# A token mixer and expert kernel on one core: the results of experts 0 to 6 go through DRAM rows instead of one-hot products

## What is computed

```python
def moe_swiglu(x, router, w1, w3, w2):
    logits = (xt @ router).astype(jnp.float32)
    top_val, top_idx = lax.top_k(logits, TOP_K)           # 2 of 8
    gate = jax.nn.softmax(top_val, axis=-1)
    combine = einsum("tk,tke->te", gate, one_hot(top_idx, 8))
    for e in range(8):
        out = out + combine[:, e:e+1] * swiglu(xt, w1[e], w3[e], w2[e])
    return out
# afterwards: h = layer_norm(ALPHA * h + out), which is the result
```

## Time and profile before

| | |
|---|---|
| median of three runs | 1586.84 us (1585.2 to 1588.51) |
| span of the profiled execution, which is its own time from first to last instruction | 1584.4 us |
| TensorE matmul busy | 1543.7 us, 97% |
| VectorE busy | 1342.3 us, 85% |
| ScalarE busy | 964.6 us, 61% |
| GpSimd busy | 47.1 us, 3% |
| moved by DMA | 446.33 MB, 282 GB/s over the span |

### The profile page before, as it was taken

The page is one execution under the profiler, slowest core; times in us unless marked ns, Lnnn a source line. Parts: engine busy times, 40 slices in busy tenths (PEclk is TensorE's granted clock), DMA queues, the critical chain, the costliest instruction groups (busy, mean ns, idle before and its releaser), DMA issues.

```text
span 1584.4 us, 18355 instructions
## 1 busy us (share of the span) xinstructions
PE 1543.7 (97%) x7468; PEld 1225.3 (77%) x7468; DVE 1342.3 (85%) x1437; ACT 964.6 (61%) x1001; POOL 47.1 (3%) x34
## 2 busy tenths in 40 slices
PE   7999999999999999999999999999999999999997
PEld 5565589989666677888888888888888888888885
DVE  8999667766599768888889989889998988998897
ACT  3233465644112537777777677677677677677775
POOL 0111000000021000000000000000000000000000
PEclk9999999999999999999999999999999999999999
DMA  8132545653442557999889999989999989999981
GB/s 338 62 151 80 213 177 200 252 205 116 186 159 80 194 205 301 377 375 359 350 345 366 359 369 365 354 340 368 356 367 372 355 340 372 369 369 371 363 334 52
DMA packets 41819, 446.33 MB, mean 282 GB/s; under 512 B 4472, under 2 KB 4728, under 8 KB 8576
## 3 DMA queue, kind: packets, MB, share of 16 engines
q1 hardware_dynamic: 39504, 438.78, 71.1%
q10 hardware_dynamic: 2224, 6.31, 1.1%
HBM read 439.81 MB, written 5.26 MB: 281 GB/s over the span
## 4 chain that ended last, share of the span: by engine, by line
PE 79%; DVE 15%; ACT 4%; issue 1%; DMA 0%; SPq 0%; DVEq 0%
PE bank L1148 36%; PE bank L1175 16%; PE bank L1033 8%; PE bank L1043 4%; PE bank L856 4%; PE bank L656 2%; DVE ring_lo L2211 2%; PE bank L1156 1%; DVE ring_lo L2354 1%; PE bank L648 1%; ACT ex_up_hi L1502 1%; PE bank L1096 1%; PE bank L1119 1%; ACT ex_w_hi L1631 1%; DVE ring L2053 1%
## 5 line engine op out<-in xcount | busy, mean ns | idle before, releaser
L2211 DVE TENSOR_TENSOR ring_lo<-ring,ex_up_hi 128x2048 fp32r<-128x2048 f32 x224 | 513.0, 2291 | 51.1 <-ACT ex_up_hi L1502 49.6
L1502 ACT ACTIVATE ex_up_hi<-ring 128x2048 fp32r<-128x2048 f32 x224 | 429.2, 1916 | 105.8 <-PE bank L1148 105.8
L1148 PE MATMUL bank<-ex_up_hi,ex_x_hi 128*128 128x512 f32 x896 | 362.4, 404 | 5.7 <-DVE ring_lo L2211 4.8
L1148 PE MATMUL bank<-ring_lo,ex_x_hi 128*128 128x512 f32 x896 | 350.6, 391 | 0.0
L1148 PE MATMUL bank<-ex_up_hi,ex_x_lo 128*128 128x512 f32 x896 | 349.9, 390 | 0.0
L2354 DVE TENSOR_TENSOR ring_lo<-ring,ex_w_hi 128x2048 fp32r<-128x2048 f32 x111 | 253.3, 2282 | 0.0
L1631 ACT ACTIVATE ex_w_hi<-ring 128x2048 fp32r<-128x2048 f32 x111 | 211.5, 1905 | 0.0
L1148 PEld LDWEIGHTS bank<-ex_up_hi,ex_x_hi 128*128 128x128 f32 x896 | 168.3, 188 | 43.9 <-DVE ring_lo L2211 12.4
L1148 PEld LDWEIGHTS bank<-ring_lo,ex_x_hi 128*128 128x128 f32 x896 | 168.2, 188 | 36.4
L1148 PEld LDWEIGHTS bank<-ex_up_hi,ex_x_lo 128*128 128x128 f32 x896 | 168.8, 188 | 30.5
L1175 PE MATMUL bank<-ex_w_hi,ex_mid_hi 128*128 128x512 f32 x448 | 174.5, 389 | 0.0
(11 more groups left out here) (362 smaller groups left out, 2041.0 us busy)
## 6 DMA issues: line engine op xcount, KB each, us to landing
ring<-moe SPq DMA_DIRECT2D x112, 2048.0 KB, 7.6
ring<-moe SPq DMA_DIRECT2D x112, 1024.0 KB, 7.4
ring<-ffn SPq DMA_DIRECT2D x11, 3072.0 KB, 10.8
win<-w_in SPq DMA_DIRECT2D x12, 2048.0 KB, 11.9
win<-w_out SPq DMA_DIRECT2D x4, 2048.0 KB, 8.0
lnb<-ln SPq DMA_DIRECT2D x4, 1024.0 KB, 6.3
tab<-yT ACTq DMA_DIRECT2D x8, 512.0 KB, 5.2
ring<-tab SPq DMA_DIRECT2D x1, 3072.0 KB, 10.1
```

The source lines that it names most:

```text
L1148: ins = mm(b[:, :], ex_x[x % 3][x_][:, k, :], (ex_up_hi, lo)[w_][:, k, :], start=(k == 0 and m == 0), stop=(k == KT - 1 and m == 2))
L1502: act(ex_up_hi[:, HS * q:HS * (q + 1), :], wt[:, HS * q:HS * (q + 1), :], ACT.Copy).then_inc(e_uh, 1)
L2211: tt(ring_lo[s][:, half], ring[s][:, half], hi.bitcast(F32), ALU.subtract).then_inc(e_ul, 1)
```

## The change

Experts 0 to 6 no longer use `take_y_lo`, `placing`, `scatter`, `add`, `placed`; only expert 7 still does (`scatter_last`; its `placing` stays at c = 7 of expert 6). Instead:

- `take_y` (still c = 1 of the next expert) copies the banks to `y_row`, in float32, and GpSimd stores it (512 KB) to rows 128 x to 128 x + 127 of a DRAM tensor `rows`. Row 896 is zero and stands for "no such row". ScalarE's copy of the next result first waits for that store.
- `row_numbers` on VectorE, in chunk 5 of expert 0: for each token the two row numbers and the two weights, 12 small instructions.
- In expert 7 GpSimd waits for all stores and then fetches the tokens' rows with four indexed transfers of 128 rows (512 KB each), n = 0 to 3, into two buffers; the third waits for the first add, the fourth for the second.
- `add_rows` on VectorE in expert 7, at c = 6, 7, 9 and 10: `acc += weight * rows`, 128x1024 in SBUF, after a wait for the transfer; each also waits for its own end.
- `gather` no longer waits for adds.

```diff
+            def expert_rows(b):
+                for x in range(b * NE, b * NE + NE - 1):
+                    po.wait_ge(e_y, 2 * x + 2)
+                    po.dma_start(rows[x % NE * P:(x % NE + 1) * P, :], y_row).then_inc(e_st, 16)
+                po.wait_ge(e_st, 16 * ((NE - 1) * (b + 1) + 1))
+                po.wait_ge(e_at, b + 1)
+                for n in range(4):
+                    if n >= 2:
+                        po.wait_ge(e_ra, 4 * b + n - 1)
+                    po.indirect_dma_start(
+                        out=row_home[n % 2], out_offset=None, in_=rows[:, :],
+                        in_offset=bass.IndirectOffsetOnAxis(ap=row_at[:, n:n + 1], axis=0)
+                        ).then_inc(e_row[n % 2], 16)
...
@@ pe: all_experts
-                    else:
-                        placing(x0)
-                    if x > x0 and c in (3, 5):
-                        scatter(x - 1, c - 3)
-                    if x % 2 == 0:
-                        if c == 7:
-                            placing(x + 1)
-                    elif x < x0 + NE - 1:
-                        if c == 7:
-                            pe.wait_ge(e_acc, 4 * x)
-                        if 7 <= c < 11:
-                            gather((x + 1) // 2, c - 7)
-                        if c == 11:
-                            placing(x + 1)
+                    if x % 2 and x < x0 + NE - 1 and 7 <= c < 11:
+                        gather((x + 1) // 2, c - 7)
+                    if x == x0 + NE - 2 and c == 7:
+                        placing(x + 1)
@@ scalar: take_y
+                e, b = x % NE, x // NE
+                ac.wait_ge(e_st, 16 * ((NE - 1) * b + e + 1))
+                if e == NE - 1:
+                    ac.wait_ge(e_ra, 4 * (b + 1))
+                home = y_hi if e == NE - 1 else y_row
@@ vector
+            def add_rows(b, n):
+                t, j = n // 2, n % 2
+                ve.wait_ge(e_row[j], 16 * (2 * b + t + 1))
+                stt(out=acc[:, t, :], in0=row_home[j], scalar=row_gate[:, t, j:j + 1], in1=acc[:, t, :],
+                    op0=ALU.mult, op1=ALU.add).then_inc(e_ra, 1)
+                ve.wait_ge(e_ra, 4 * b + n + 1)
@@ vector: all_experts
-                    if c == 2 and x > x0:
-                        take_y_lo(x - 1)
-                    if c in (4, 6) and x > x0:
-                        add(x - 1, c - 4)
-                    if x % 2 == 0:
-                        if c == 8:
-                            placed(x + 1)
-                    elif x < x0 + NE - 1:
+                    if i == 5:
+                        row_numbers()
+                    if x % 2 and x < x0 + NE - 1:
                         if c == 6:
-                            ve.wait_ge(e_tm, x + 1)
+                            ve.wait_ge(e_g, 4 * ((x + 1) // 2))
                             prepare((x + 1) // 2)
...
+                    if x == x0 + NE - 2 and c == 8:
+                        placed(x + 1)
+                    if x == x0 + NE - 1 and c in ADDED:
+                        add_rows(b, ADDED.index(c))
```

More of the change, by code:

```diff
@@ L86, with trunk @@
     ("ret_gn", 2), ("ml_gn", 2), ("s5_d", 2), ("hy_b1", 1), ("hy_b2", 1), ("hy_freq", 1)])
-def trunk(nc, x, ln, const, par, w_in, w_out, ffn, moe, tab, out):
+def trunk(nc, x, ln, const, par, w_in, w_out, ffn, moe, tab, rows, out):
     ctx = ExitStack()
@@ L154, in trunk @@
         pick_x = over_sb("pick_x", "sc", 1024, [P, TT, 2 * P])
-        place = [over_sb(f"place{i}", "sc", 1536 + i * 256, [P, L]) for i in range(2)]
+        place = over_sb("place", "sc", 1536, [P, L])
+        y_row = yT[:, :, :].rearrange("p k n -> p (k n)")[:, 0:D]
+        row_home = [pr[:, 2 * D:3 * D], y_row]
+        row_at = over[:, 4:8]
         bank = [ctx.enter_context(nc.psum_tensor(f"bank{i}", [P, 512], F32)) for i in range(8)]
@@ L254, in trunk @@
         rt1 = vo[:, 448:456]
+        row_base = vo[:, 456:464]
+        row_gate = vo[:, 464:468].rearrange("p (t j) -> p t j", j=2)
+        row_pos = vo[:, 468:472].rearrange("p (t j) -> p t j", j=2)
+        row_of = cmp1[:, :, 0:2, :]
+        row_ok, row_n = cmp2[:, :, 0, :], cmp2[:, :, 1, :]
         sil = [sc[:, i * 256:(i + 1) * 256] for i in range(2)]
@@ L330, in trunk @@
         e_yl, q_hi, q_lo = sem("ex_y_split"), sem("moe_h_hi"), sem("moe_h_split")
+        e_st, e_at, e_ra = sem("zero_row_and_ex_rows_stored"), sem("row_numbers"), sem("ex_rows_added")
+        e_row = [sem(f"ex_rows_fetched{i}") for i in range(2)]
         e_lh, e_ll, e_dh = sem("ex_last_w2_hi_half"), sem("ex_last_w2_half"), sem("ex_last_down_half")
@@ L537, in _ @@
                     nc.gpsimd.tensor_tensor(hrstd, hvar, mhalf, ALU.pow).then_inc(n_rstd, 1)
+            po.wait_ge(q_pos, 1)
+            po.wait_ge(h_ready, 8)
+            nc.gpsimd.memset(pr[0:1, 2 * D:3 * D], 0.0).then_inc(pch, 1)
+            po.wait_ge(pch, 1)
+            po.dma_start(rows[(NE - 1) * P:(NE - 1) * P + 1, :], pr[0:1, 2 * D:3 * D]).then_inc(e_st, 16)
+            def expert_rows(b):
[11 more added lines that the diff above has]
+                        ).then_inc(e_row[n % 2], 16)
+            expert_rows(0)
+            po.wait_ge(q_px, 2)
+            crowded = po.value_load(over[0:1, 0:1], min_val=0, max_val=1)
+            with po.If(crowded == 1):
+                expert_rows(1)
         @block.tensor
@@ L1089, in gather @@
                     pe.wait_ge(e_p, m + 1)
+                if m % 4:
+                    pe.wait_ge(e_xg, 4 * m + q - 1)
                 elif q >= 2:
@@ L1107, in placing, with scatter_last @@
                 ins.then_inc(e_tm, 1)
[L1109 to L1117, removed]
-                    for n, part in enumerate((y_hi, y_lo)):
[L1119 to L1125, removed]
-                pe.wait_ge(e_acc, 4 * x)
[L1127 to L1130, removed]
+            def scatter_last(x):
+                pe.wait_ge(e_t, x // NE + 1)
+                pe.wait_ge(e_xg, 4 * (x // 2) + 4)
+                for (t, hf), b in zip(LAST, LAST_BANK):
+                    pe.wait_ge(e_yl, x // NE * 2 + hf + 1)
+                    for n, part in enumerate((y_hi, y_lo)):
+                        ins = mm(bank[b][:, :], place[:, t * P:(t + 1) * P], part[:, hf * 512:(hf + 1) * 512],
                                  start=(n == 0), stop=(n == 1))
@@ L1166, in down @@
                 pe.wait_ge(e_mid, g + 1)
+                if c == 0 and x >= 2:
+                    pe.wait_ge(e_y, 2 * (x - 1))
                 lo = ring_lo[MOE_SLOTS[g % SLOTS]]
@@ L2320, in placed, with row_numbers @@
             def placed(x):
-                ve.wait_ge(e_tm, x + 1)
[L2322 to L2329, removed]
+                ve.wait_ge(e_tm, x // NE + 1)
+                nc.vector.tensor_copy(place[:, :], bank[6][:, 0:L]).then_inc(e_t, 1)
+            def row_numbers():
+                of_e, rank = posx[:, :, 0:NE], rt[3]
+                link(ts(row_base, K("iota")[:, 0:NE], float(P), -float((NE - 1) * P), ALU.mult, ALU.add))
+                link(ts(row_ok, of_e, -0.5, None, ALU.is_gt))
+                link(stt(out=row_ok, in0=of_e, scalar=P - 0.5, in1=row_ok, op0=ALU.is_lt, op1=ALU.mult))
+                link(tt(row_n, of_e, bc(row_base, 1, TT), ALU.add))
+                link(tt(row_n, row_n, row_ok, ALU.mult))
+                for j in range(2):
+                    ins = stt(out=row_of[:, :, j, :], in0=rank, scalar=float(j), in1=row_n,
+                              op0=ALU.is_equal, op1=ALU.mult)
+                link(ins)
+                link(nc.vector.tensor_reduce(row_pos, row_of[:, :, :, 0:NE - 1], AX.X, ALU.add))
+                ts(row_at, row_pos.rearrange("p t j -> p (t j)"), float((NE - 1) * P), None, ALU.add).then_inc(e_at, 1)
+                for j in range(2):
+                    ins = stt(out=row_of[:, :, j, :], in0=rank, scalar=float(j), in1=comb[:, :, 0:NE],
+                              op0=ALU.is_equal, op1=ALU.mult)
+                link(ins)
+                link(nc.vector.tensor_reduce(row_gate, row_of[:, :, :, :], AX.X, ALU.add))
+            def add_rows(b, n):
[4 more added lines that the diff above has]
+                ve.wait_ge(e_ra, 4 * b + n + 1)
             def x_lo(m, q):
@@ L2445, in all_experts @@
                         up_lo(g + 1, 1, after)
[L2446 to L2449, removed]
+                    if i == 0 and not b:
+                        crowded.append(ve.value_load(over[0:1, 0:1], min_val=0, max_val=1))
                 w2_lo_half(b * CH + CH - 1, 1)
@@ L2583 @@
     out = nc.dram_tensor("out", [L, D], F32, kind="ExternalOutput").ap()
-    trunk(nc, *args, tab, out)
+    rows = nc.dram_tensor("rows", [(NE - 1) * P + 1, D], F32, kind="Internal").ap()
+    trunk(nc, *args, tab, rows, out)
     r = _run(nc, [arrays], core_ids=[0])
```

21 lines of the change are left out of this document (8 added, 13 removed).

## The result

The changed kernel took 1565.09 us (median of four runs, 1564.17 to 1565.78) and the kernel before, beside it, 1586.02 us (1583.91 to 1588.51). The ratio is 0.9869, with a 95% interval of 0.9858 to 0.9881. The forecast was 1566.5 us in a range of 1563 to 1578. A second measurement, on another occasion, gave a ratio of 0.9872 (0.9856 to 0.9889).

The account below looks back on a forecast made before the run. The prediction took TensorE to bound a plain chunk, with DMA waiting for it. 21.5 us removed less 0.4 for adds and 0.8 for row numbers gave 20.3 us, so 1586.8 became 1566.5 us, range 1563 to 1578.

Parts of the forecast that it names:

- What is removed: Extras in the intervals of experts 0 to 7: 21.5 us goes, about 14 TensorE's own work, 7.5 late starts by VectorE.
- The 1.3 us that VectorE has free: Plain chunk, ahead of `up_lo`: VectorE can take about 1.3 us more before TensorE waits.
- `prepare` alone: Interval 6 of odd experts: `prepare`, 0.69 us, fits in VectorE's free time, so the 0.72 us extra goes whole.
- The row numbers: Chunk 5 of expert 0: 12 small VectorE instructions, 2.1 us less 1.3 free, cost 0.8 once; bounds 0.4 and 1.6.
- The adds: Four `add_rows` in expert 7: 0.1 us each, 0.4 in all; bounds 0 and 0.6 each.
- the signs: What the changed profile should show; among them intervals 6, 7, 9 and 10 of expert 7 within 0.2 of plain.
- The transfers: Seven stores and four fetches, 5.8 MB: cost 0; fetch time bounded by 5.2 and 15 us, some 28 us free.
- Rival 1: DMA becomes the bound in the experts: some 13 us lost, 7 of the gain left, 1579 us; chance 0.09.
- Rival 2: GpSimd's descriptor making holds VectorE at the 11 transfers: 12 us at most, half likely, 1572 us; chance 0.08.
- Rival 3: Indexed fetches come too late for `add_rows` in expert 7: slower, 1597 us if one takes 42 us; chance 0.07.
- Rival 4: The change doesn't do what it says: second pass would have to run, or products stay; given no chance of its own.
- the forecast's own bounds: Whole kernel: 1563 us below; 1571 above, from dearer adds and row numbers, start and spread; chance 0.76.

Follow-up runs that it names:

- dve_free: Changed kernel with VectorE's old pairs of instructions put back at c = 2, 4 and 6 of experts 1 to 7, without waits, writing to two places; 1573.05 us.
- dve_kept: Changed kernel with VectorE's old pairs of instructions put back at c = 2, 4 and 6 of experts 1 to 7, each followed by a wait for itself; 1578.99 us.
- again: The changed kernel run once more, no edit; 1566.26 us, ratio 0.9872 to the kernel before.
- spread: Changed kernel with row numbers split over chunks 5, 7, 9 of expert 0 and adds at c = 5, 7, 9, 11 of expert 7; 1564.66 us.
- stores5: Changed kernel with each expert's result stored five times, to five places; 1566.74 us.
- adds_early: Changed kernel with the four adds of fetched rows at c = 3, 4, 6 and 7 of expert 7; 1572.17 us.
- after: The changed kernel itself, in its first measurement and profile; 1565.09 us.
- pe_kept: Changed kernel with eight unused matmuls put back on TensorE in chunks 3 and 5 of experts 1 to 7; 1577.4 us.
- no_transfers: Changed kernel without the seven stores and four indexed fetches, the adds reading whatever lies in the buffers; 1566.22 us.
- spread_b: Second run of the changed kernel with row numbers in three parts and adds at c = 5, 7, 9, 11; 1564.63 us.

## Why the prediction was right, point by point

**What is removed** was to be 21.5 us, 14 of it TensorE's own. The runs put TensorE's `scatter` at 12.74 (12.6 expected), `placing` at 0.25 each, and the whole at 21.8. Reading single intervals was what made this work: by busy time VectorE has 19 us less to do and TensorE 19 (1543.7 to 1524.9), and neither number nor their sum tells which part of it was hidden.

**The 1.3 us that VectorE has free** in a plain chunk carried three terms, and it was about 0.1 too large. The prediction counted up to the start of the first `up` matmul, 922.07; its weight load waits for the low parts too and starts 0.22 us earlier. In the kernel before:

```profile
921.85 0.19 PEld L1148 LDWEIGHTS bank<-ex_up_hi,ex_x_hi 128*128 128x128 f32 x1
```

Part of it comes back, since a VectorE instruction that waits for nothing starts 0.08 us before the one ahead ends (731.03 against 730.43 + 0.68 in `dve_free`). The runs agree on 1.2 us, counted from start to start: 1.32 us of added work cost 0.11 (interval 4 of expert 2 in `dve_free`), 1.57 cost 0.35 (`dve_kept`), and the 2.13 of the row numbers cost 0.93. `prepare` alone fits: interval 6 of expert 1 is 8.43 (`again`: 8.41), for 9.14 before. The row numbers cost 0.93 for 0.8, by this 0.1; cut to three pieces of under 0.9 us they cost nothing (`spread`). The adds cost 0.11, 0.23, 0.11 and 0.16, 0.61 for 0.4 in the first profile, near the lower end, as argued from the place of ScalarE's copy; the 0.23 is just outside the 0.2 that the signs allowed.

**The transfers** cost 0, as forecast. A store's landing was mis-sized, on the unsafe side, by 1.7 us of the 28 that were free: 6.9 us, where the nearest row had 5.2. The list of DMA issues of the changed kernel gives the fetches 9.7 us (into `pr`) and 11.8 us (into `yT`), each the median of two and within the bounds of 5.2 and 15:

```profile
pr<-rows,over POOLq DMA_INDIRECT x2, 9.7
yT<-rows,over POOLq DMA_INDIRECT x2, 11.8
```

The 3.2 us estimated from the Trainium skill's DMA: Bandwidth & Descriptors, section "Anatomy of one DMA — SWDGE (gpsimd) path", are half of what the stores took; all of them ran beside the weight loads, and no run here shows one alone.

**Rival 1** (DMA) fell: 396 GB/s in `stores5` with even and odd experts no longer than in `again`. **Rival 2** (GpSimd and VectorE) fell: with or without transfers 946.6. The contention of the earlier trace rows is real for GpSimd's adds; descriptors showed none of it. **Rival 3** (late fetches) is true as a mechanism and was far from its point: in the changed kernel the first fetch was ready about 20 us ahead of its add, the third and the fourth 12 to 13. Its price, one for one, was too low once TensorE stood still for long: in `adds_early` the clock added 1.7 us. **Rival 4** played no part.

**The sum.** Gain 20.3 forecast, 20.9 between the medians and 20.2 in the second measurement. In the first pair of profiles 18.6 of 20.7 came from the stretch and 2.3 from before it, with 0.3 lost behind; in the second profile the stretch alone gave 20.5. That the first pair of spans matches so well is in part luck: a start that was 2.3 us earlier and plain intervals that were 0.02 us longer nearly cancel. The terms missed by a little in both directions as well, 21.8 for 21.5 removed and 1.6 for 1.2 added. What failed is small: the plain interval, which I took as 8.42 in both kernels, was 8.434 or 8.413 by execution; the free time was 1.2 us; and the upper end of the forecast's own bounds adds up to 1572, not 1571.

## What to carry to other kernels

Find an event that comes once in each pass of a loop, and read the passes one by one: each extra then stands in its own pass, already net of what was hidden. Measure how much free time the second engine has ahead of the instruction that the first waits for. Work below that costs nothing, what passes it costs one for one, and the same work cut into pieces and put in several passes costs nothing again. A result that is needed much later can go through DRAM, and the transfers themselves cost nothing while DMA keeps up, provided that the last fetch isn't put close behind the last store.

## What the runs showed of the hardware that I had not expected

A wait of a VectorE instruction for itself, put between two others, costs about 0.12 us: two of them moved the next start from 1.20 to 1.45 us. Over 21 chunks their removal brought the cost of VectorE's old work from 14.1 to 8.6 us.

An idle stretch of TensorE of 4.9 us (`adds_early`) was followed by 3.3 us near the lower clock, which cost 1.7 us more; behind one of 1.7 us (`stores5`) the clock stayed at 1.00. A late wait can thus cost more than its length.

The plain interval has two lengths, 8.413 and 8.434 us, with the same instructions. In `after` and `spread` the longer one held through experts 0 to 6 and ended in expert 6; in `pe_kept` and `stores5` it ended after four intervals and in `dve_kept` after seven; `again`, `no_transfers`, `adds_early` and `spread_b` had it in single intervals at most, and the kernel before has both lengths mixed. It goes with the execution and not with the kernel, since `spread` and `spread_b` are one program. These two ran on different chips; but `stores5` and `adds_early`, on the chip of `spread`, didn't hold it, so the chip alone doesn't set it either. What sets it stays open.
